# Two hybrid decoder layers on one core: the chunk inverse on four quarters of TensorE throughout, and U times the values in one step

## The reference, cut to what matters

```
L = einsum('bhnid,bhnjd->bhnij', k_beta, k) * decay(tri_strict)
T = triangular_solve(eye + L, eye)            # 64 x 64 per head and chunk
u = T @ v_beta
w = T @ (k_beta * exp(g))
a_intra = einsum('bhnid,bhnjd->bhnij', q, k) * decay(tri_incl)
def step(state, xs):                          # over the 4 chunks, in order
    v_new = u_c - w_c @ state
    o = (q_c * exp(g_c)) @ state + a_c @ v_new
    state = state * exp(gl) + einsum('bhcd,bhce->bhde', k_dec, v_new)
```

## Time and profile before

| | us |
|---|---|
| median of 3 runs | 1910.38 (1908.45 to 1911.38) |
| profiled execution | 1906.44 |
| its span | 1904.6 |
| TensorE busy | 1723.9 (91%) |
| VectorE busy | 1391.3 (73%) |
| ScalarE busy | 905.9 (48%) |
| granted TensorE clock, mean | 0.993 |

### The profile page before, as it was taken

The page is one execution under the profiler, slowest core; times in us unless marked ns, Lnnn a source line. Parts: engine busy times, 40 slices in busy tenths (PEclk is TensorE's granted clock), DMA queues, the critical chain, the costliest instruction groups (busy, mean ns, idle before and its releaser), DMA issues.

```text
span 1904.6 us, 26678 instructions
## 1 busy us (share of the span) xinstructions
PE 1723.9 (91%) x7264; PEld 996.9 (52%) x7264; DVE 1391.3 (73%) x3891; ACT 905.9 (48%) x2237; POOL 689.7 (36%) x585
## 2 busy tenths in 40 slices
PE   8999999999999787777799999999999997878786
PEld 7987887544444232222289778865544442322232
DVE  5885758977778777776469847689777787777754
ACT  5555643444445454444355555435444444444443
POOL 0110003453444556656311100034444444566553
PEclk9999999999999999999999999999999999999999
DMA  6532689999999999999955326899999999999997
GB/s 246 186 117 84 188 313 369 423 427 426 427 426 399 424 419 427 428 427 427 415 186 171 120 92 193 317 406 420 426 427 427 426 403 425 422 428 427 428 427 303
DMA packets 106730, 660.61 MB, mean 347 GB/s; under 512 B 11888, under 2 KB 12288, under 8 KB 40064
## 3 DMA queue, kind: packets, MB, share of 16 engines
q0 software_dynamic: 75376, 546.57, 68.7%
q1 hardware_dynamic: 31248, 112.74, 17.5%
HBM read 658.20 MB, written 1.06 MB: 346 GB/s over the span
## 4 chain that ended last, share of the span: by engine, by line
PE 38%; DMA 22%; issue 22%; DVE 10%; ACT 5%; POOL 1%; DVEq 1%; POOLq 0%; ACTq 0%; SPq 0%
PE acc L846 11%; DMA arena<-experts_dram,idxu 10%; DMA arena<-experts_dram,stage 7%; DMA cst<-experts_dram,stage 5%; PE acc L865 4%; PE psum L715 3%; DVE arena L1670 3%; PE psum L716 3%; PE psum L717 3%; PE psum L778 2%; PE psum L746 2%; PE acc L715 1%; DVE arena L1493 1%; PE acc L716 1%; PE acc L717 1%
## 5 line engine op out<-in xcount | busy, mean ns | idle before, releaser
L865 PE MATMUL acc<-arena 128*128 128x512 f32 x896 | 440.2, 620 | 118.8 <-ACT arena L1311 118.5
L846 PE MATMUL acc<-arena 128*128 128x512 f32 x896 | 411.1, 601 | 27.7 <-ACT arena L1285 27.4
L677 POOL DMA_INDIRECT arena<-experts_dram,stage x224 | 306.5, 1368 | 221.6 <-PE acc L865 166.4
L1700 DVE CUSTOM_DVE_ANT_0 arena<-arena,h 128x1024 f32<-128x1024 f32 x224 | 274.5, 1226 | 134.6 <-issue 58.3
L865 PEld LDWEIGHTS acc<-arena 128*128 128x128 f32 x896 | 158.0, 193 | 398.4 <-issue 398.3
L659 POOL DMA_INDIRECT arena<-experts_dram,idxu x224 | 245.9, 1098 | 301.5 <-PE acc L846 272.0
L1670 DVE CUSTOM_DVE_ANT_0 arena<-arena,h 128x1024 f32<-128x1024 f32 x224 | 274.6, 1226 | 103.1 <-DMA arena<-experts_dram,idxu 99.3
L846 PEld LDWEIGHTS acc<-arena 128*128 128x128 f32 x896 | 163.3, 190 | 254.4 <-issue 154.8
L1554 DVE TENSOR_TENSOR raw_r<-raw,w_hi_r 128x1024 fp32r<-128x1024 f32 x150 | 177.8, 1220 | 79.4 <-ACT w_hi_r L1187 78.3
L1305 ACT ACTIVATE gel<-dots 128x1 f32<-128x1 f32 x256 | 51.7, 202 | 295.5 <-DVE dots L1700 294.7
L1187 ACT ACTIVATE w_hi_r<-raw 128x1024 fp32r<-128x1024 f32 x152 | 154.0, 1052 | 56.9 <-DMA raw<-weights_dram 56.7
(11 more groups left out here) (297 smaller groups left out, 2772.3 us busy)
## 6 DMA issues: line engine op xcount, KB each, us to landing
raw<-weights_dram SPq DMA_DIRECT2D x168, 512.0 KB, 3.6
arena<-weights_dram SPq DMA_DIRECT2D x20, 512.0 KB, 5.6
w_hi<-weights_dram SPq DMA_DIRECT2D x12, 512.0 KB, 6.6
lnr<-lnrows_dram POOLq DMA_DIRECT2D x4, 1024.0 KB, 6.5
arena<-experts_dram,idxu POOLq DMA_INDIRECT x224, 13.1
arena<-experts_dram,stage POOLq DMA_INDIRECT x224, 13.5
lnr<-cum_dram POOLq DMA_DIRECT2D x2, 1024.0 KB, 9.1
cst<-weights_dram SPq DMA_DIRECT2D x4, 512.0 KB, 5.3
```

The costliest lines, as they stand in the source:

```text
L677: nc.gpsimd.indirect_dma_start(slots[i % RING][:, :], None, experts[:, :], bass.IndirectOffsetOnAxis(stage[:, i:i + 1], 0)).then_inc(slot_ ...
L846: last = mm(acc[:, c * 512:(c + 1) * 512], diag[:, i % 4, :], slots[n % RING][:, D + c * 512:D + (c + 1) * 512], start=n == 0, stop=n == R ...
L865: last = mm(acc[:, c * 512:(c + 1) * 512], diag[:, i % 4, :], slots[i % RING][:, D + c * 512:D + (c + 1) * 512], start=False, stop=ends)
L1700: nc.vector.tensor_tensor_reduce(slots[i % RING][:, 0:D], slots[i % RING][:, 0:D], h[:, b, :], 1.0, 0.0, ALU.mult, ALU.add, dots[:, i:i + ...
```

## The change: what it does

- `t0`, `y` and the last `uy` run on four quarters: block 0 writes the half it reads, block 1 the other half. The two steps of a kind now are the blocks b, not the chunks c: a bank holds both chunks of one block. ACT drains block 0 with one copy of 128 partitions and block 1 with two copies of 64, which cross the halves.
- In levels 1 to 4 `ty` is one step with one bank and `uy` another (before two banks each). DVE adds `ty` in one instruction of 128 partitions, `uy` in two of 64.
- A new step pair `uv` after the inverse: U times values of all four chunks, 16 products of 64 x 64 x 128, on four quarters, block b in bank b. ACT copies them into `vnew` in four instructions of 64 x 512.
- `vn` keeps only the product with the state; chunk 0 has none. DVE, not ACT, drains it, by adding it into `vnew`.

```
-        s += [("y", lev, c) for c in range(2)] + attend(lev - 1) + gated(1) + exponentials(lev - 1)
-        s += [(k, lev, c) for k in (("ty", "uy") if lev < LEVELS - 1 else ("uy",)) for c in range(2)] + gated(2)
-    s += [("wT", 0), ("wT", 1)] + attend(5)
+        s += [("y", lev, b) for b in range(2)] + attend(lev - 1) + gated(1) + exponentials(lev - 1)
+        s += ([("ty", lev), ("uy", lev)] if lev < LEVELS - 1 else [("uy", lev, b) for b in range(2)]) + gated(2)
+    s += [("uv", 0), ("uv", 1), ("wT", 0), ("wT", 1)] + attend(5)
...
+        def new_values(L, n):
+            return (vnew_ready, 3 * L + n) if n else drained(L, ("uv", 0))
...
+            def across(L, banks, left, right, swap, width=CHUNK):
+                for hd in range(GH):
+                    cs = slice(hd * CHUNK, (hd + 1) * CHUNK)
+                    for b in range(2):
+                        for c in range(2):
+                            rows, made = half_rows(c), half_rows(1 - c if swap[b] else c)
+                            at_b = b * T if width == CHUNK else 0
+                            to = slice(at_b + hd * width, at_b + (hd + 1) * width)
+                            yield mm(bank(L, banks[b])[made, to], left[rows, b, cs], right(rows, b, cs), start=True, stop=True)
...
+            def chunk_inverse(L, step):      # waits for banks and operands, then
+                if kind == "t0":
+                    products = across(L, made, Um, lambda rows, b, cs: cident[rows, :], (0, 1))
+                elif kind == "y":
+                    products = across(L, made, Xm, lambda rows, b, cs: Tm[rows, b, cs], (0, 1))
+                elif kind == "uv":
+                    products = across(L, made, Um, lambda rows, b, cs: vb[rows, b, 2 * cs.start:2 * cs.stop], (0, 1), P)
+                elif kind == "uy":
+                    products = across(L, made, Ym, lambda rows, b, cs: Um[rows, b, cs], (0, 1))
+                else:
+                    t_products = across(L, [step] * 2, Um, lambda rows, b, cs: Ym[rows, b, cs], (0, 0))
+                    u_products = across(L, made[1:] * 2, Ym, lambda rows, b, cs: Um[rows, b, cs], (1, 1))
+                    products = itertools.chain.from_iterable(zip(t_products, u_products))
...                                            # TensorE, vn
+                        if n == 0:
+                            pe.sem_inc(bank_filled[bk], 1)
+                            continue
...
-                            last = mm(ps[0:CHUNK, cs], Um[rows, b, own], vb[rows, b, cs], start=not n, stop=True, skip_group_check=True)
...                                            # ScalarE
-                    elif kind == "vn":
-                        AC(vnew[rows, b, :], ps[0:CHUNK, :], ACT.Copy).then_inc(vnew_ready, 1)
+                    elif kind == "uv":
+                        b = step[1]
+                        for c in range(2):
+                            last = AC(vnew[half_rows(c), b, :], ps[half_rows(1 - c if b else c), :], ACT.Copy)
...                                            # VectorE
+                        if kind == "ty":
+                            last = TT(Tm, Tm, made, ALU.add)
...
+                    elif kind == "vn":
+                        if b + c:
+                            TT(vnew[rows, b, :], vnew[rows, b, :], ps[0:CHUNK, :], ALU.add).then_inc(vnew_ready, 1)
```

More of the change, by code:

```diff
@@ L640, in _ @@
                         pool.wait_ge(*dense_consts(L))
-                        for c in range(2):
-                            pool.wait_ge(*filled(L, ("y", step[1], c)))
+                        for b in range(2):
+                            pool.wait_ge(*filled(L, ("y", step[1], b)))
                         for b in range(2):
@@ L792, in turn @@
                 last.then_inc(bank_filled[bk], 1)
[L794 to L804, removed]
-                    if level > 1:
[L806 to L815, removed]
@@ new lines, in chunk_inverse @@
+            def chunk_inverse(L, step):
+                kind = step[0]
+                level = 0 if kind in ("t0", "uv") else step[1]
+                made = [step, ("uy", level)] if kind == "ty" else [step[:-1] + (b,) for b in range(2)]
+                for st in made:
+                    bk, use = place(L, st)
+                    if use:
+                        pe.wait_ge(bank_drained[bk], use)
+                if kind == "t0":
+                    pe.wait_ge(*dense_consts(L))
+                    pe.wait_ge(u_init, L * NB + NB)
+                elif kind == "y" and level == 1:
+                    pe.wait_ge(x1_ready, L * NB + NB)
+                    for b in range(2):
+                        pe.wait_ge(*drained(L, ("t0", b)))
+                elif kind == "y":
+                    pe.wait_ge(x_ready, (L * (LEVELS - 2) + level - 1) * NB)
+                    pe.wait_ge(*drained(L, ("ty", level - 1)))
+                elif kind == "uv":
+                    for b in range(2):
+                        pe.wait_ge(*drained(L, ("uy", LEVELS - 1, b)))
+                else:
+                    for b in range(2):
+                        pe.wait_ge(*drained(L, ("y", level, b)))
+                    if level > 1:
+                        pe.wait_ge(*drained(L, ("uy", level - 1)))
+                if kind == "t0":
+                    products = across(L, made, Um, lambda rows, b, cs: cident[rows, :], (0, 1))
+                elif kind == "y":
+                    products = across(L, made, Xm, lambda rows, b, cs: Tm[rows, b, cs], (0, 1))
[3 more added lines that the diff above has]
+                    products = across(L, made, Ym, lambda rows, b, cs: Um[rows, b, cs], (0, 1))
+                else:
+                    t_products = across(L, [step] * 2, Um, lambda rows, b, cs: Ym[rows, b, cs], (0, 0))
+                    u_products = across(L, made[1:] * 2, Ym, lambda rows, b, cs: Um[rows, b, cs], (1, 1))
+                    products = itertools.chain.from_iterable(zip(t_products, u_products))
+                products = list(products)
+                ends[0], ends[1] = products[-2 if kind == "ty" else -3], products[-1]
+                ends[0].then_inc(bank_filled[place(L, step)[0]], 1)
@@ L927, in _ @@
                         continue
[L928 to L931, removed]
+                    if kind in ("t0", "y", "ty", "uy", "uv"):
+                        if step[-1] == 1 and kind != "ty" or kind == "uy" and step[1] < LEVELS - 1:
+                            ends[1].then_inc(bank_filled[place(L, step)[0]], 1)
+                        else:
+                            chunk_inverse(L, step)
                         continue
@@ L938, in _ @@
                         continue
-                    both = kind in ("t0", "y", "ty", "uy", "wT", "fs", "fv", "gate") or kind == "out" and step[1] == 0 or kind == "br" and step[1:3] != (2, 1)
+                    both = kind in ("wT", "fs", "fv", "gate") or kind == "out" and step[1] == 0 or kind == "br" and step[1:3] != (2, 1)
                     blocks = [(ps, step[-1])]
@@ L1030, in _ @@
                                 last = mm(ps[c * CHUNK:(c + 1) * CHUNK, hd * CHUNK:(hd + 1) * CHUNK], fT[:, b, 2, cs], fT[:, b, 3, cs] if kind == "lt" else qw[:, b, 0, 2 * hd + c, :], start=True, stop=True)
[L1031 to L1047, removed]
+                    elif kind == "wT":
+                        for b in range(2):
+                            pe.wait_ge(*drained(L, ("uy", LEVELS - 1, b)))
                         for b in range(2):
@@ L1051, in _ @@
                                 for ps2, c in blocks:
[L1052 to L1063, removed]
+                                    rows = half_rows(c)
+                                    ends[c] = mm(ps2[:, b * T + hd * CHUNK:b * T + (hd + 1) * CHUNK], kbe[rows, b, hd * P:(hd + 1) * P], Um[rows, b, cs], start=True, stop=True)
                     elif kind == "vn":
@@ L1068, in _ @@
                         pe.wait_ge(*drained(L, ("wT", c)))
[L1069 to L1074, removed]
+                        if n == 0:
+                            pe.sem_inc(bank_filled[bk], 1)
+                            continue
+                        pe.wait_ge(*drained(L, ("dS", (n - 1) // 2, (n - 1) % 2)))
                         for hd in range(GH):
-                            cs, own = slice(hd * P, (hd + 1) * P), slice(hd * CHUNK, (hd + 1) * CHUNK)
-                            last = mm(ps[0:CHUNK, cs], Um[rows, b, own], vb[rows, b, cs], start=not n, stop=True, skip_group_check=True)
+                            cs = slice(hd * P, (hd + 1) * P)
+                            t0 = (2 * hd + c) * P
+                            last = mm(ps[:, cs], pairs[:, b, t0:t0 + P], Sm[:, n % 2, cs], start=hd == 0, stop=False, skip_group_check=True)
                     elif kind == "dS":
@@ L1401, in _ @@
                         last = AC(to, made, ACT.Copy)
[L1402 to L1407, removed]
+                    elif kind in ("t0", "y"):
+                        b = step[-1]
```

(29 more changed lines are left out.)

13 lines of the change are left out of this document (7 added, 6 removed).

## The result

| | before | changed |
|---|---|---|
| median, us | 1910.51 (4 runs) | 1896.70 (4 runs, 1895.92 to 1898.16) |
| profiled execution / span | 1906.44 / 1904.6 | 1895.92 / 1894.1 |
| ratio of times | | 0.993, 95% interval 0.9918 to 0.9941 |

The changed kernel is 13.8 us faster by the medians; the interval is 11.3 to 15.7 us. The forecast was 1898.2 by the median and 1894.2 for the profiled execution. The interval holds the 12.2 us of the sum and the time lies in the range.

The account below looks back on a forecast made before the run. TensorE was taken to bound the mixer, bytes moved the experts. Per layer 3.5 + 3.0 - 0.4 = 6.1 us, 12.2 in two layers, took the median from 1910.38 to 1898.2 us; range 1894.5 to 1903.5.

Parts of the forecast that it names:

- What bounds it: In the mixer TensorE is full and weight loads follow it, so a microsecond saved there is one of the span, per layer.
- Part 1: Inverse in the mixer: `t0`, `y` and last `uy` on four quarters, seven steps per layer saving 0.5 us each, 3.5 us.
- the variant with a fixed part: Step estimate in the inverse: 31 x 0.015 + 0.15 = 0.62 us for 32 instructions, against 0.54 if nothing is fixed.
- Part 2: Mixer: U times values moved out of `vn` into `uv`, 4.07 us becoming 1.05, 3.0 us saved per layer.
- Part 3: ACT's copies and DVE's adds in the inverse stay covered by TensorE's work: cost 0, or 0.5 us per step if uncovered.
- New waits: Behind the inverse, `fs` and `o` of chunk 1 wait for ACT or DVE: 0.4 us per layer, bounds 0 to 1.5.
- The sum: Both mixers: 3.5 + 3.0 - 0.4 = 6.1 us saved per layer, 12.2 in two layers; forecast chance 0.76.
- The range: Whole kernel: the forecast's own range was 9 to 13.6 us saved; the stated range of times was 1894.5 to 1903.5 us.
- Rival C: Inverse and `uv`: products of a block's two chunks take turns in their shared bank, 5.4 us slower, 1915.8; chance 0.08.
- the rule: Skill statement on PSUM in the mixer's products: different row halves cannot access one bank at the same time; no size itself.
- B: Recurrence or inverse: DVE or ACT becomes last, losing 2 us per layer; 8.2 us gained in all, 1902.2; chance 0.09.
- D: Behind the mixer something has its own time, so the span does not follow: gain 0 to 3 us, 1907.4 to 1910.4; chance 0.07.

## Why the prediction was right, step by step

- **What bounds it.** Right. A microsecond of TensorE in the mixer was a microsecond at the first gather, both ways: with parts taken back and with `y` three times, and the medians moved with it.
- **Part 1, 3.5 us per layer.** Right in kind, a little high. A step takes 0.63, not 0.58: the variant with a fixed part (0.62) was the true one and I took the middle. 7 x 0.45 = 3.15; undoing it cost 3.18 and 3.16.
- **Part 2, 3.0 us per layer.** `uv` 1.04 against 1.05 is right, and four quarters do run at once at 128 columns. What was mis-sized is the removal: I charged 1.02 per chunk, the row of L1077 alone. `vn` of chunks 1 to 3 went from 2.00 to 0.80 us, since the step behind the product with the state starts 0.18 sooner when it is `wide` and not a 64 x 64 product. Chunk 0's 1.01, three times 1.20, less 1.04: 3.57 us, 0.6 more than the sum had.
- **Part 3, no cost.** Right in effect. ACT's copies of one `y` take 0.39 + 0.77 = 1.16 us, not 0.9, but they lie under other steps as expected; DVE's adds of one level take the 2.1 us counted.
- **New waits, 0.4 us.** 0.51, at the place, on the instruction and by the queue named; the maximum ended 1.4 us behind the product where I had 1.3. `fs` waited for nothing, the lag did not reach chunk 2. Of the lag of 1.4 us, 0.5 went with two of ACT's copies; the 0.9 that stayed is put down to the small product gone, which no run tried alone.
- **The sum, 6.1 per layer.** 3.15 + 3.57 - 0.51 = 6.21, measured 6.22 and 6.24 up to `o`. That the forecast came so near is in part luck: part 1 was 0.35 too high and part 2 0.57 too low. The 1.5 us between forecast and median are no finding either: the profiled execution missed its 1894.2 by 1.7 us to the other side.
- **The range.** Its lower end was added up wrong. With waits of 1.5 and `uv` 1 us dearer the terms give 2 x (6.3 - 1.5 - 1.0) = 7.6 us, not 9. Nothing hung on it here.
- **Rival C and the rule.** The 64-instruction pair stayed at 1.09 us with both row halves ending in one bank, and `y` went to 0.63 in the same layout, where taking turns would have made them 2.16 and 1.08. The Trainium skill, TensorEngine Tiling (Array Packing), Gotcha 1: PSUM Pressure, says that row halves cannot access one PSUM bank at the same time; where they write the two partition halves of the bank, this trace shows no such limit. The Trainium skill, PSUM — Partial Sum Buffer, "PSUM bank collisions raise a hardware error", reports as measured, for two engines, that accesses to different 32-partition quadrants of one bank do not collide; for products of two row halves of TensorE the trace agrees (0.63 and 1.09 us).
- **B** kept 0.5 of its 2 us per layer; **D** nothing.

## What to carry to other kernels

When an engine is full and the DMA queue waits for it, price an edit by the distances between starts on that engine and nothing else, and then ask which drain has just lost its cover. Price the removal of a small product by the distance from the step before it to the step after it, not by its own row: the neighbour's end may hang on it. On a full TensorE, products that use a part of the array are worth issuing side by side wherever what they read and what they write can lie in different halves: here 32 instructions went from 1.08 to 0.63 us, and ACT's copies of them took no longer (1.16 us against 1.21).

## What the runs showed of the hardware

- Steps of 64 x 64 x 64 f32 products on four quarters took 0.63, 1.09 and 1.56 us for 32, 64 and 96 instructions: 14.5 ns each and 0.17 us fixed. On two quarters 32 took 1.08. A quarter's own pace is about 58 ns, whether two or four are at work.
- The step behind eight full-array instructions started 0.98 us after the first of them when it was a 64 x 64 product and 0.80 us when it was `wide`. The eight stand (1.05 - 0.27) / 7 = 0.11 us apart, so by their own pace the next would start at 0.89: half of the 0.18 us is the small product coming 0.09 late, the other half is `wide` coming 0.09 early. Behind `wide` a 64 x 64 product comes late by as much: 0.32 us after its last instruction (159.88 to 160.20), where two `wide` instructions stand 0.23 apart. The Trainium skill, TensorEngine Tiling (Array Packing), Key Properties, says that a change of tiling mode drains TensorE; the rows agree with a cost, and it is about 0.1 us here.
